# Two scan steps, three weight pieces and the gate of z are moved in a two-layer hybrid step; the ring of weight slots is used longer in full

## The reference, cut to what matters

```
y_off = einsum('bclhn,bchpn,bhcl->bclhp', cm, h_enter, exp(cs))   # per chunk of 128 tokens
y     = y_f + rev(y_b) + xs * d_skip
out   = rmsnorm(y * silu(z), ssm_g)
mod   = silu(c) @ w_ada[l] + b_ada[l]                             # 1024 x 6144, in pieces
```

## Time and profile before

| | |
|---|---|
| median of three runs | 774.4 us |
| profiled execution, its own time | 772.91 us |
| span of the profiled execution | 771.1 us |
| TensorE busy | 739.3 us (96%) |
| VectorE busy | 581.4 us (75%) |
| ScalarE busy | 506.7 us (66%) |
| GpSimd busy | 50.4 us (7%) |
| granted TensorE clock, mean | 0.996 |

### The profile page before, as it was taken

One profiled execution on the slowest core, in us unless ns is written; L12 is line 12 of the kernel. 1 busy time (PEld: TensorE's weight loads), 2 busy tenths in 40 slices (PEclk: granted clock), 3 DMA queues, 4 the chain that ended last, 5 costly groups with the idle time before them and its releaser, 6 DMA issues.

```text
span 771.1 us, 10986 instructions
## 1 busy us (share of the span) xinstructions
PE 739.3 (96%) x4022; PEld 573.3 (74%) x4022; DVE 581.4 (75%) x964; ACT 506.7 (66%) x842; POOL 50.4 (7%) x36
## 2 busy tenths in 40 slices
PE   5999999899999999999999999988999999999994
PEld 2558877458967888888878888845798888888884
DVE  4268386987566899999878746789767799998965
ACT  3048693584557877877655778457556787777854
POOL 0001342000000000000000134200000000000000
PEclk9999999999999999999999999999999999999998
DMA  9963034977338999999854203095831299999902
GB/s 348 424 275 110 14 122 156 424 269 299 110 117 355 371 362 365 378 376 356 307 224 178 87 23 131 7 389 211 318 119 55 69 333 376 376 364 375 370 28 86
DMA packets 34062, 186.22 MB, mean 241 GB/s; under 512 B 5200, under 2 KB 6608, under 8 KB 17104
## 3 DMA queue, kind: packets, MB, share of 16 engines
q1 hardware_dynamic: 34000, 185.42, 63.4%
HBM read 182.79 MB, written 2.62 MB: 240 GB/s over the span
## 4 chain that ended last, share of the span: by engine, by line
PE 78%; DVE 10%; ACT 7%; issue 4%; DMA 0%; DVEq 0%; ACTq 0%; SPq 0%
PE psum L905 23%; PE psum L934 12%; PE psum L1067 12%; PE psum L1269 5%; PE psum L1032 4%; PE psum L883 3%; PE psum L724 3%; PE psum L966 3%; DVE att L2341 1%; PE psum L787 1%; PE psum L1239 1%; PE psum L1137 1%; ACT split L1473 1%; PE psum L918 1%; PE psum L1151 1%
## 5 line engine op out<-in xcount | busy, mean ns | idle before, releaser
L2130 DVE TENSOR_TENSOR split<-ring,split 128x2048 fp32r<-128x2048 f32 x96 | 219.8, 2290 | 23.3 <-ACT split L1608 21.8
L1608 ACT CAST split<-ring 128x2048 fp32r<-128x2048 f32 x96 | 183.5, 1912 | 21.4 <-PE psum L934 14.8
L905 PE MATMUL psum<-split,y_hi 128*128 128x512 f32 x512 | 161.0, 395 | 0.0
L905 PEld LDWEIGHTS psum<-split,y_hi 128*128 128x128 f32 x512 | 93.6, 188 | 18.2
L905 PE MATMUL psum<-split,y_lo 128*128 128x512 f32 x256 | 100.1, 391 | 0.0
L1067 PE MATMUL psum<-ring_r,hT_hi 128*128 128x512 f32 x216 | 73.2, 393 | 0.0
L934 PE MATMUL psum<-split,hidT 128*128 128x512 f32 x256 | 69.7, 394 | 0.0
L934 PEld LDWEIGHTS psum<-split,hidT 128*128 128x128 f32 x256 | 47.3, 188 | 12.4 <-DVE hidT_lo L2135 2.7
L905 PEld LDWEIGHTS psum<-split,y_lo 128*128 128x128 f32 x256 | 48.0, 188 | 10.2
L2572 POOL TENSOR_TENSOR ud<-const,da_hi 128x1024 fp32r<-128x1024 f32 x12 | 27.3, 2293 | 390.6 <-DVE da_lo L2231 383.1
L1067 PEld LDWEIGHTS psum<-ring_r,hT_hi 128*128 128x128 f32 x216 | 40.0, 188 | 9.0 <-issue 0.8
(11 more groups left out here) (324 smaller groups left out, 1430.2 us busy)
## 6 DMA issues: line engine op xcount, KB each, us to landing
ring<-in_w_gu SPq DMA_DIRECT2D x64, 1024.0 KB, 5.0
ring<-in_w_ada SPq DMA_DIRECT2D x40, 1024.0 KB, 6.7
ring<-in_w_down SPq DMA_DIRECT2D x32, 1024.0 KB, 5.1
ring<-in_w_rows SPq DMA_DIRECT2D x12, 1024.0 KB, 5.0
ring<-in_w_out SPq DMA_DIRECT2D x8, 1024.0 KB, 5.2
ring<-in_first SPq DMA_DIRECT2D x7, 1024.0 KB, 17.2
ring<-in_w_xbc SPq DMA_DIRECT2D x8, 800.0 KB, 8.9
par<-in_par SPq DMA_DIRECT2D x1, 1728.0 KB, 16.3
```

What stands on the lines that cost most here:

```text
L905: last = pe.matmul(dst, x[:, g, t, :], w[:, j, :], start=(t == 0 and i == 0), stop=(t == KD - 1 and i == 2))
L1608: act.copy(splits[unit_split(n)][:, 0, :], slot(key)).then_inc(raised("whi", l, p), 1)
L2130: tt(lo, slot(unit_key(l, p, n)), hi.bitcast(F32), ALU.subtract).then_inc(raised("wlo", l, p), 1)
```

## The change

1. In each layer (ssm_y, 2) stands ahead of rows 5, and (ssm_off, 1) and (ssm_off, 2) stand together behind rows 5 of tile 0.
2. Three pieces are multiplied between the z rows: after rows 4 of tile 1, after rows 4 of tile 2, after rows 5 of tile 0. The rest is spread evenly over the heads.
3. The slots 0 to 2 are withheld from (scores, 6) on instead of from (scores, 0). The planner takes the slots of the halves of h and of rows 5 as used three pieces later than it did.
4. The Silu of z is replaced. For each tile ScalarE takes exp(-z) (gate_in), GpSimd clips it and adds 1, ScalarE takes Ln and then Exp of the negative (gate_sigmoid), and GpSimd multiplies z by it. gate_in(0) and gate_sigmoid(0) lie in the z rows, gate_in(1) behind rows 5 of tile 1, gate_in(2) before scores(1), gate_sigmoid(1) and (2) before scores(3) and scores(4). gate(m) waits for GpSimd. No other table is loaded for it.
5. The banks of the moved products are named: beyond_rows(l, n) is the n-th bank after that of z's row of tile 0.

```diff
-    s += [("ssm_y", 1), ("ssm_in", 2), ("w_split", 5), ("rows", 4, 0), ("seg", 2), ("rows", 4, 1), ("rows", 4, 2), ("turn_qk", 1), ("prep", 2)]
-    s += [("rows", 5, m) for m in range(TILES)] + [("ssm_y", 2), ("silu_z",)]
-    burst = 6 if l else 3
-    s += ada[early:burst]
+    s += [("ssm_y", 1), ("ssm_in", 2), ("w_split", 5), ("rows", 4, 0), ("seg", 2), ("rows", 4, 1), ada[early], ("rows", 4, 2), ada[early + 1],
+          ("turn_qk", 1), ("prep", 2)]
+    s += [("ssm_y", 2), ("rows", 5, 0), ("gate_in", 0), ada[early + 2], ("ssm_off", 1), ("ssm_off", 2), ("gate_sigmoid", 0)]
+    s += [("rows", 5, 1), ("gate_in", 1), ("rows", 5, 2)]
+    spent = early + AHEAD_OF_SCORES
     heads = head_steps()
-    at = heads.index(("scores", 2))
-    heads[at:at] = [("ssm_off", 1)]
-    at = heads.index(("scores", 3))
-    heads[at:at] = [("ssm_off", 2)]
+    at = heads.index(("scores", 1))
+    heads[at:at] = [("gate_in", 2)]
+    for m in (1, 2):
+        at = heads.index(("scores", m + 2))
+        heads[at:at] = [("gate_sigmoid", m)]
...
-    rest = ada[burst:8] + [("ada_turn", l, 1)] + ada[8:14]
+    rest = ada[spent:8] + [("ada_turn", l, 1)] + ada[8:14]
...
-        want = min(len(rest), len(rest) * (i + 1) * 3 // (len(heads) * 2)) if i < len(heads) // 3 else \
-            len(rest) // 2 + (len(rest) - len(rest) // 2) * (i + 1 - len(heads) // 3) // (len(heads) - len(heads) // 3)
+        want = len(rest) * (i + 1) // len(heads)
...
-            if s == ("scores", 0):
+            if s == ("scores", PAIRS // 2):
                 first_late = len(pieces)
...
+        if key[0] == "w_hi" and key[2] == 5:
+            for i, k in enumerate((("h_hi", key[1], 0), ("h_hi", key[1], 1), key, ("win", key[1], 5))):
+                last_use[place[k]] = n + AHEAD_OF_SCORES + 0.1 * (i + 1)
...
+        def beyond_rows(l, n):
+            return (uses["row", l, 0, 2][0] + n) % 7
...
-                        pe.wait_ge(*fill(("ydiag", l, m)))
+                        pe.wait_ge(*fill(("ydiag", l, m), beyond_rows(l, 1) if m == 2 else None))
...
-                        pe.wait_ge(*fill(("state", l, m)))
+                        pe.wait_ge(*fill(("state", l, m), beyond_rows(l, 2) if m == 2 else None))
...
-                            pe.wait_ge(*fill(("yoff", l, m, g)))
+                            pe.wait_ge(*fill(("yoff", l, m, g), beyond_rows(l, (5, 6, 1, 2)[2 * m - 2 + g])))
...
+                        turn[0] = beyond_rows(l, 4)
...
-                    elif kind == "silu_z":
-                        for m in range(TILES):
-                            act.wait_ge(*taken(("row", l, m, 2)))
-                        act.activation(z, z, ACT.Silu).then_inc(sig["zs"], 1)
-                        act.preload_act_table_set("natural_log_exp_and_others")
+                    elif kind == "gate_in":
+                        m = arg[0]
+                        act.wait_ge(*taken(("row", l, m, 2)))
+                        act.wait_ge(*full(("ydiag", l, 2)))
+                        act.wait_ge(*full(("state", l, 2)))
+                        act.activation(z_exp[:, m, :], z[:, m, :], ACT.Exp, scale=-1.0).then_inc(sig["z_act"], 1)
+                    elif kind == "gate_sigmoid":
+                        m = arg[0]
+                        act.wait_ge(sig["z_pool"], per["z_pool"] * l + 2 * m + 1)
+                        act.activation(z_exp[:, m, :], z_exp[:, m, :], ACT.Ln).then_inc(act_step, 1)
+                        act.wait_ge(act_step, act_steps())
+                        act.activation(z_exp[:, m, :], z_exp[:, m, :], ACT.Exp, scale=-1.0).then_inc(sig["z_act"], 1)
...
-                        dve.wait_ge(sig["zs"], per["zs"] * l + 1)
+                        dve.wait_ge(sig["z_pool"], per["z_pool"] * l + 2 * m + 2)
...
+                    if step[0] == "gate_in":
+                        m = step[1]
+                        pool.wait_ge(sig["z_act"], per["z_act"] * l + 2 * m + 1)
+                        pool.tensor_scalar(z_exp[:, m, :], z_exp[:, m, :], 1e30, 1.0, ALU.min, ALU.add).then_inc(sig["z_pool"], 1)
+                    elif step[0] == "gate_sigmoid":
+                        m = step[1]
+                        pool.wait_ge(sig["z_act"], per["z_act"] * l + 2 * m + 2)
+                        tt(z[:, m, :], z[:, m, :], z_exp[:, m, :], ALU.mult).then_inc(sig["z_pool"], 1)
```

More of the change, by code:

```diff
@@ L52 @@
 LAST = ((0, 2), (2, 4), (4, 6), (6, 7), (7, 8))
+AHEAD_OF_SCORES = 3
 SCRATCH = 1024
@@ L455, in build @@
                 m_lo = sb("m_lo", [P, 4, TOK], F32R, c=after_state)
+            with ExitStack() as after_last_state:
+                z_exp = sb("z_exp", [P, TILES, DS], c=after_last_state)
             xs = sb("xs", [P, DS], c=mix)
@@ L549, in build @@
                 ("dt_r", 1), ("da", 1), ("bss", 3), ("brs", 3), ("prep", 3), ("ud", 3), ("ud_lo", 3), ("da_lo", 1), ("xd", 3), ("yx", 3),
-                ("mhi", 4), ("mlo", 4), ("mixhi", 4), ("ohi", 1), ("olo", 1), ("wb", 3), ("dtd", 1), ("skip", 3), ("seg", 6), ("in_hi", PARTS + 2), ("in_lo", PARTS + 3), ("zs", 1), ("nb", PAIRS), ("es", PAIRS // 2), ("pn", PAIRS), ("yz", 1), ("yrs", 1), ("yn", 1),
+                ("mhi", 4), ("mlo", 4), ("mixhi", 4), ("ohi", 1), ("olo", 1), ("wb", 3), ("dtd", 1), ("skip", 3), ("seg", 6), ("in_hi", PARTS + 2), ("in_lo", PARTS + 3), ("z_act", 6), ("z_pool", 6), ("nb", PAIRS), ("es", PAIRS // 2), ("pn", PAIRS), ("yz", 1), ("yrs", 1), ("yn", 1),
                 ("flag", 1), ("top", 2), ("shares", 2), ("chosen", 2), ("hhi", 6),
@@ L2392, in _ @@
                     elif kind == "gate":
-                        dve.wait_ge(sig["zs"], per["zs"] * l + 1)
+                        m = arg[0]
+                        dve.wait_ge(sig["z_pool"], per["z_pool"] * l + 2 * m + 2)
                         dve.wait_ge(*taken(("ydiag", l, 0)))
-                        m = arg[0]
                         ins = tt(y[:, m, :], y[:, m, :], z[:, m, :], ALU.mult)
```

## The result

The changed kernel takes 778.5 us (median of 7 runs, 777.6 to 780.8) against 774.4 for the one before (7 runs, 772.7 to 776.1): ratio 1.0046, 95% interval 1.0030 to 1.0062. Forecast were 769.3 us and a range up to 773.4; the kernel became slower, by 3.6 us or so, where 5.1 were to be won. The profiled execution is the slowest of the seven, 780.8 us.

The account below looks back on a forecast made before the run. VectorE was taken to hold the first half of the heads. Of TensorE's gaps, gains of 2.4 us in layer 0 and 2.6 in layer 1, together 5.1 with rounding, gave 774.4 - 5.1 = 769.3 us; range 766.0 to 773.4.

Parts of the forecast that it names:

- So no wait by itself: GpSimd's part in z's gate: ScalarE and VectorE would not wait for it, products being done 5 us or more before.
- hand count: Layer 1's heads, timed from the scores' start: gate_sigmoids before exponentials leave TensorE 1.4 us of waits; 0.3 in layer 0.
- the slower rival: GpSimd's tensor_scalar is long; decides once three operations hold VectorE over 1.8 us each; 780.0 us, chance 0.08.
- The granted clock is 1.00 throughout, so no term comes from it.: TensorE's clock in the z rows and heads: at full speed, so priced at nothing.
- TensorE's sum is unchanged by the move.: Moving ssm_off out of the heads into the z rows adds no TensorE time.
- The heads: TensorE's gaps there, 3.44 and 4.93 us, would fall to 1.0 in layer 0 and 2.3 in layer 1.
- VectorE's relief: Moving ssm_off out of the heads frees VectorE, which holds their first half, of 5.4 us a layer.
- VectorE's busy share in the first half: In the first half of the heads it would fall from 0.9 to about 0.7 or 0.75.
- The lock: GpSimd's three operations in each layer's heads hold VectorE through the shared port; as rival, about 774.4 us, chance 0.06.
- the prep chain ahead of it does not move: VectorE's work before hin keeps its times, so ssm_off(1) has 0.3 us of slack and costs 0.
- Their going saves nothing: Removing z's 1.48 us Silu and its table loads gains nothing, since the first exponentials wait for VectorE anyway.
- 0.8 and 0.5: Microseconds of TensorE's waits for pieces not yet landed, which the new slots would remove.

Follow-up runs that it names:

- e1: Changed kernel with the gate's semaphore counts numbered in the order its steps really come; ratio 0.9994 to the kernel before.
- e2: As e1, with GpSimd's clipping and addition left out and 1 added inside ScalarE's Ln; ratio 0.9975 to the kernel before.
- e9: As e2, with ssm_off(1) and ssm_off(2) back between the scores in the heads; ratio 1.0087 to the kernel before.
- e8: As e2, with each layer's three pieces together right ahead of ssm_off(1) instead of between z rows; 772.3 us, ratio 0.9972 to the kernel before.
- e11: As e8, with the product of z and its sigmoid on VectorE instead of GpSimd; ratio 1.0011 to the kernel before.
- e4: Kernel before with only the scan's move (ssm_y(2) ahead of rows 5, both ssm_off behind tile 0's row); ratio 1.0108 to the kernel before.
- e5: As e2, with the three pieces together behind rows 5 of tile 2 instead of between the z rows; ratio 1.0026 to the kernel before.
- e12: As e8, with the old Silu of z and its table loads behind z's last row; ratio 1.0090 to the kernel before.
- e7: As e2, with the ring's slots as before the change; ratio 1.0105 to the kernel before.
- e10: Changed kernel, wrong counts kept, with one piece of w_ada of layer 1 placed in front of turn(3); ratio 1.0044 to the kernel before.

## Why the prediction was wrong, point by point

The forecast was 769.3 us, 5.1 below the kernel before; the change came out 3.6 above. About half of the difference is one step of the prediction that was wrong in kind, the waits of z's gate. Two further terms, the cost of switching and the gaps left in the heads, were too small.

*z's gate and GpSimd: here it failed.* "So no wait by itself" and the hand count "gate_sigmoid(1) 7.0, pair 3 7.7, turn(1)'s copy 8.1, gate_sigmoid(2) 9.4" took it that each wait is met by its own tile's signal. The semaphore counts something else. This costs 4.5 us (e1), and the diff that the prediction had before it shows it; it was read for what is computed, not for which signal is the fifth. The two-step tensor_scalar takes 1.92 us, inside the bounds of the earlier trace rows but not the 1.04 taken: more than the 1.8 from which the slower rival was to decide. Yet by itself (e1 against e2) it costs 0.35 by the stretch, so that rival isn't what happened, though its 780.0 us lie close to the result. In the wrong order the 1.92 lie on the path in full.

*"The granted clock is 1.00 throughout, so no term comes from it."* True of the kernel before, and wrong as a reason. Two waits close together halved the clock behind them: 2.2 of layer 1's 4.2 us are busy time that goes with e1, and 2.7 of e9's 7.3. A priced wait can carry this with it.

*"TensorE's sum is unchanged by the move."* Not so. The z rows should have taken 21.52 us + 2.05 for ssm_off (24.65 in e2 less 22.6 in e9), in layer 1 with one piece of 0.9 more, 23.6 in both; they took 24.65. 1.0 us a layer goes into changes from one kind of matmul to another: 0.66 for the pieces' scattering (e8). The other 0.4 is still there in e8. It is not ssm_off's: e9, with ssm_off out of the rows, has 22.6 against 21.52 before, the whole 1.1. What is left is ssm_y(2) and one block between the rows, which no run separates. That is 2.1 us of the 5.1.

*The heads.* With right counts (e1) the gaps by windows are 42.19 - 39.60 = 2.59 and 39.64 - 36.53 = 3.11 us against 1.0 and 2.3 forecast, down from 3.44 and 4.94. VectorE's relief is real (e9), but it went to layer 1, where the turns' waits for the scaling of hT fell from 3.0 to 1.5. In layer 0 they rose, from 0.8 to 1.7 after, 2.1 in e1 and 1.8 in e2 and e8. One wait of 0.86 us after lies behind GpSimd's product (see below); what holds the others stays open. VectorE's busy share in the first half was to fall to 0.70 or 0.75; after, it is 20.13 of 23.89 us in layer 0, 0.84, and 18.83 of 23.81 in layer 1, 0.79, part of that time spent standing behind GpSimd.

*The lock.* 521.36, 1.53 us for a scaling of usually 0.48, ending 0.1 behind GpSimd's product; and at 524.46 a 128x2 operation of usually 0.16 took 1.03, until that product's end at 525.47. In layer 0 the same operation took 1.26 at 148.91, beside the product from 148.88 on, and TensorE waited 0.86 us for the scaling behind it. The Trainium skill ("SBUF — State Buffer", section "Who interferes with whom") has the shared pair locked for a whole instruction; the trace agrees, down to the smallest operation with two inputs in SBUF. Yet taking GpSimd out (e11) was worse: the lock costs less than VectorE's own three products. For VectorE the lock's size can be read: in the heads it is busy 33.77 and 32.53 us in e1 and 32.52 and 32.13 in e4, where GpSimd does nothing there, 1.25 and 0.40 us less. How much of that TensorE sees, put down as 1.0, no run separates.

*What held, in part by luck.* hin comes just in time. VectorE's last update of it, and TensorE's ssm_off(1) with its first matmuls of hin, in layer 0 after (answering to the earlier trace rows):

```profile
127.32 0.56 DVE L2269 TENSOR_TENSOR row<-row,nrm 128x384 f32<-128x384 f32 x1 [1.11 <-ACT nrm L1738]
131.58 0.42 DVE L2335 TENSOR_TENSOR hin<-psum,hin 128x256 f32<-128x256 f32 x1
...
132.39 0.71 PE L1191 MATMUL psum<-par,xbc 64*128 64x256 f32 x4
132.93 1.13 PE L1191 MATMUL psum<-hin,xbc 64*128 64x256 f32 x8
```

There is no wait, and the pieces ahead are why (1.9 us in e4 and e5). The slack is 132.39 - 132.00 = 0.4 us, for 0.3 forecast. But both sides came 1.0 us later than forecast, counted from seg(2): "the prep chain ahead of it does not move" was wrong, since prep(2) now waits 1.11 us for ScalarE's nrm, which stands behind its copy of turn_qk(1)'s result. TensorE came late by its switching. The two delays cancel. ssm_y(2) doesn't wait. The landings go, ada_turn's 1.1 us in layer 0 too; in layer 1 it is 0.5 for 0.3. Exp and Ln take 0.63 us, for 0.6 taken from the earlier trace rows.

*What was too small.* "Their going saves nothing" and "0.8 and 0.5": each edit was priced against the order of before. In the new order the Silu costs 10 us (e12, against e8) and the old slots 9.5 (e7, against e2), both by the stretch. The parts of this change lean on one another: the scan's move alone is 8 us slower (e4). The slots and the gate were not tried alone on the order of before.

Put together, by the stretch: forecast -5.1; counts +4.5 (half of it busy time at the lower clock), switching +2.1, gaps larger in the heads 5.70 - 3.3 = +2.4, comes to +3.9; the stretch is 3.95 longer, and the timed ratio says +3.6.

## What to carry to other kernels

Where a step list gives the order and waits are written as a formula of an index, write out the semaphore's sequence beside the steps before pricing any of it: a count that is one too high shows only as a stall. A wait on TensorE can cost twice, once by its length and once by the matmuls at half rate behind it; here this was so behind two waits close together and behind one of 4.0 us. Put filler right ahead of the wait that it covers: moved away from it, it cost 2.7 us (e5). One block instead of three pieces saved 1.4 us by the stretch (e8), which the times don't resolve.

## What the hardware showed

- GpSimd's tensor_scalar of two steps on 128x512 takes 1.92 us (2.23 at most), its product of two tensors 1.26 to 1.42. The first reads one tensor and does two operations on it (min, add). The Trainium skill ("GPSIMD Engine Reference", section "Engine selection") calls one input roughly line rate and two about twice as slow; in this case it is the other way round.
- With 2.07 of 4 us busy, the clock held in the profile of the changed kernel and fell to 0.53 in that of e10, at the same steps of layer 0; behind a single wait of 4.0 us (e12) it was 0.50, behind one of 1.48 with a piece ahead (e10) it stayed at 1.00.
- Alternating kinds of matmul costs TensorE about 0.33 us for each visit of a block between rows, there and back: 0.66 us a layer for two blocks of eight matmuls set between rows instead of together with a third.
